# Turning the latents in 32x32 blocks on VectorE instead of on TensorE

## The reference, cut to what matters

```python
proj = jnp.einsum('bsd,dn->bsn', xn, w_in[l])
a_q, a_k, a_v, a_g, b_cq, b_ckv, b_kr, b_g = jnp.split(proj, _SPLITS, axis=-1)
...
c_q = rms_norm(b_cq, b_cq_norm[l])
c_kv = rms_norm(b_ckv, b_ckv_norm[l])
qb = jnp.einsum('bsr,rn->bsn', c_q, w_uq[l])
kvb = jnp.einsum('bsr,rn->bsn', c_kv, w_ukv[l])
...
h = h + jnp.einsum('bsm,md->bsd', y, w_out[l])
```

## Time and profile before

| | |
|---|---|
| median of 3 runs | 1583.99 us (1583.68 to 1584.9) |
| profiled execution | 1581.66 us, its span 1579.9 us |
| TensorE products | 1534.4 us busy, 97% of the span |
| TensorE weight loads | 889.6 us, 56% |
| VectorE | 1303.0 us, 82% |
| ScalarE | 1232.3 us, 78% |
| GpSimd | 586.0 us, 37% |
| mean granted clock of TensorE | 0.997 |

### The profile page before, as it was taken

One profiled execution on the slowest core, in us unless ns is written; L12 is line 12 of the kernel. 1 busy time (PEld: TensorE's weight loads), 2 busy tenths in 40 slices (PEclk: granted clock), 3 DMA queues, 4 the chain that ended last, 5 costly groups with the idle time before them and its releaser, 6 DMA issues.

```text
span 1579.9 us, 37686 instructions
## 1 busy us (share of the span) xinstructions
PE 1534.4 (97%) x13326; PEld 889.6 (56%) x13326; DVE 1303.0 (82%) x1947; ACT 1232.3 (78%) x1656; POOL 586.0 (37%) x506
## 2 busy tenths in 40 slices
PE   7999999999998999999999999999999999979999
PEld 3555555555553566566566556656655655644444
DVE  6886676776888988998898899899889889897764
ACT  8787667667657888888888888888888888877663
POOL 0100000000002665666666566666656656630000
PEclk9999999999999999999999999999999999999999
DMA  9344444453323543334323334323332422536663
GB/s 339 109 137 76 112 116 71 109 110 70 82 65 98 112 99 72 86 82 96 79 64 92 79 79 97 86 65 70 83 66 63 92 58 67 125 91 213 201 198 106
DMA packets 245540, 162.51 MB, mean 103 GB/s; under 512 B 65040, under 2 KB 226320, under 8 KB 245488
## 3 DMA queue, kind: packets, MB, share of 16 engines
q1 hardware_dynamic: 222128, 147.28, 37.2%
q10 hardware_dynamic: 22464, 13.63, 3.1%
q0 software_dynamic: 896, 0.93, 0.8%
HBM read 119.16 MB, written 40.93 MB: 101 GB/s over the span
## 4 chain that ended last, share of the span: by engine, by line
PE 56%; DVE 8%; issue 3%; ACT 0%; DVEq 0%; DMA 0%; POOLq 0%; SPq 0%
PE p_acc L2063 5%; PE p_st L2027 5%; PE p_st L2026 5%; PE p_acc L2067 4%; DVE hand_part L1864 4%; PE hand_mx L1994 4%; PE p_acc L2069 4%; PE p_acc L2068 3%; PE p_st L1507 3%; PE p_st L1508 3%; PE p_st L1510 3%; PE p_st L2029 3%; PE p_st L2030 3%; PE hand_mx L1996 3%; PE p_acc L2064 3%
## 5 line engine op out<-in xcount | busy, mean ns | idle before, releaser
L1776 POOL TENSOR_TENSOR p_pl<-p_p,p_ph 128x512 f16<-128x512 f32 x384 | 503.9, 1319 | 291.6 <-ACT p_ph L1815 232.3
L1864 DVE TENSOR_REDUCE hand_part<-hand_mx 128x2 f32<-128x1024 f32 x373 | 455.0, 1220 | 78.1 <-PE hand_mx L1994 60.0
L1806 ACT ACTIVATE p_p<-p_st 128x1024 f32<-128x1024 f32 x384 | 390.9, 1018 | 98.3 <-PE p_st L2034 50.2
L1194 PE MATMUL p_ring<-p_w_hi,p_xT 128*128 128x512 f16 (+3 forms) x1536 | 389.3, 339 | 7.5 <-DVE p_w_lo L902 5.0
L1815 ACT ACTIVATE p_ph<-p_p 128x1024 f16<-128x1024 f32 x336 | 355.2, 1057 | 18.4
L1892 DVE TENSOR_TENSOR p_pl<-p_p,p_ph 128x512 f16<-128x512 f32 x384 | 325.9, 849 | 5.4 <-ACT p_ph L1815 4.6
L1194 PE MATMUL p_ring<-p_w_lo,p_xT 128*128 128x512 f16 (+3 forms) x768 | 260.0, 339 | 0.0
L1194 PEld LDWEIGHTS p_ring<-p_w_hi,p_xT 128*128 128x128 f16 x1536 | 150.7, 98 | 127.1 <-DVE p_xT L860 5.6
L2063 PE MATMUL p_acc<-p_vas,p_ph 128*128 128x129 f16 x2048 | 207.9, 221 | 0.0
L2063 PEld LDWEIGHTS p_acc<-p_vas,p_ph 128*128 128x128 f16 x2048 | 180.6, 97 | 36.4 <-issue 14.1
L2064 PE MATMUL p_acc<-p_vas,p_pl 128*128 128x65 f16 x2048 | 201.1, 193 | 0.0
(11 more groups left out here) (196 smaller groups left out, 2364.8 us busy)
## 6 DMA issues: line engine op xcount, KB each, us to landing
p_vbs<-scratch_vb SPq DMA_DIRECT2D x16, 1028.0 KB, 6.3
p_xin<-in_x SPq DMA_DIRECT2D x16, 512.0 KB, 7.1
p_xcol<-in_x_cols SPq DMA_DIRECT2D x16, 512.0 KB, 6.7
scratch_g<-p_g SPq DMA_DIRECT2D x16, 512.0 KB, 3.4
p_kb<-scratch_kb SPq DMA_DIRECT2D x32, 256.0 KB, 5.4
p_vas<-in_x SPq DMA_DIRECT2D x16, 512.0 KB, 4.0
out<-p_ph SPq DMA_DIRECT2D x15, 512.0 KB, 2.8
out_gt<-scratch_g ACTq DMA_DIRECT2D x13, 512.0 KB, 3.4
```

The source lines that it names most:

```text
L1194: last = pe.matmul(ring_t[:, 0:w], a, b, start=(k == 0 and m == 0), stop=(k == len(steps) - 1 and m == len(terms) - 1))
L1776: pool.tensor_tensor(pl[:, s % NP, 1, :], p32[:, s % N32, QB:], ph[:, s % NP, 1, :], ALU.subtract).then_inc(s_lop, 1)
L1806: act.activation(p32[:, s % N32, :], st[:, s % 2, :, :].rearrange("p a b -> p (a b)"), ACT.Exp, scale=scale).then_inc(s_exp, 1)
L1864: dve.tensor_reduce(part[:, e // MPAIRS % 3, 2 * c:2 * c + 2], mx[:, :, :], AX, ALU.max).then_inc(s_red, 1)
```

## The change

The latents are scaled in float32 in place (`latent_scale`, ScalarE), turned in 32x32 blocks by VectorE into `turned_lat`, a part of the tile `T2` that the rotation uses at other times (`latent_turn`), split into halves from there (`latent_hi`, `latent_lo`), and put in their places by 16 copies of 32x320, eight on each engine (`latent_move`). TensorE's `turn_latents`, the two copies from PSUM and their semaphores go. In ScalarE's queue `latent_hi` now stands behind `z_hi` and `latent_move` where `latents_turned` stood. In VectorE's, `latent_turn` stands where `latent_lo` stood, and `latent_lo` behind `x_lo`. In tiles 14 and 15 all but the moves stand ahead of `rotate_heads`.

```diff
-        lat_hi = sb("lat_hi", [P, RQ + RKV], F16)
-        lat_lo = sb("lat_lo", [P, RQ + RKV], F16)
+        lat = sb("lat", [P, 2, RQ + RKV], F16)
...
+        turned_lat = T2[:, 0:RQ + RKV]
...
-        turned_hi = ps("turned_hi", [P, 8, P], F16)
-        turned_lo = ps("turned_lo", [P, 8, P], F16)
+        turned_hi = ps("turned_hi", [P, 2, P], F16)
+        turned_lo = ps("turned_lo", [P, 2, P], F16)
...
+        def latent_moves(quadrants):
+
+            halves = lat[:, :, :].rearrange("p s (k q t) -> p (s k) q t", k=5, q=4)
+            for g, d in moves(quadrants):
+                yield latT[32 * d:32 * d + 32, :, 32 * g:32 * g + 32], halves[32 * g:32 * g + 32, :, d, :]
...
         def _(act):
-            def latents_turned(t):
-
-                act.wait_ge(s_lph, t + 1)
-                act.activation(latT[:, 0:5, :], turned_hi[:, 0:5, :], ACT.Copy).then_inc(s_lth, 1)
+            def latent_move(t):
+
+                act.wait_ge(s_dlat, t * 3 + 3)
+                if not zero(t):
+                    act.wait_ge(s_proj, turn(t - 1, "ukv1") + 1)
+                for dst, src in latent_moves((2, 3)):
+                    last = act.activation(dst, src, ACT.Copy)
+                last.then_inc(s_lta, 1)
...
+            def latent_scale(t, h):
                 ls = lstat[:, h, :]
-                act.wait_ge(s_dlat, t * 2 + 1)
+                act.wait_ge(s_dlat, t * 3 + 1)
+                act.activation(cq32[:, h, :], cq32[:, h, :], ACT.Copy, scale=ls[:, 4:5])
+                act.activation(ckv32[:, h, 0:RKV], ckv32[:, h, 0:RKV], ACT.Copy, scale=ls[:, 5:6]).then_inc(s_lat, 1)
+
+            def latent_hi(t):
+
+                act.wait_ge(s_dlat, t * 3 + 2)
                 if not zero(t):
-                    act.wait_ge(s_lph, t)
-                act.activation(lat_hi[:, 0:RQ], cq32[:, h, :], ACT.Copy, scale=ls[:, 4:5])
-                act.activation(lat_hi[:, RQ:], ckv32[:, h, 0:RKV], ACT.Copy, scale=ls[:, 5:6]).then_inc(s_lat, 1)
+                    act.wait_ge(s_lta, t)
+                    act.wait_ge(s_ltd, t)
+                act.activation(lat[:, 0, :], turned_lat, ACT.Copy).then_inc(s_lat, 1)
...
                 latent_stat(t, h)
-                latent_hi(t, h)
+                latent_scale(t, h)
                 if not last:
                     z_hi(t - 1, 1 - h)
+                    latent_hi(t)
                     x_hi(t + 1, 1 - h)
                     aq_out(t, h)
                     akv_out(t, h)
-                    latents_turned(t)
+                    latent_move(t)
                     z_move(t - 1, 1 - h, i if h == 1 else i - 1)
                     gate(t, "ag")
                 elif h == 0:
+                    latent_hi(T14)
                     aq_out(T14, 0)
                     akv_out(T14, 0)
                     z_hi(T13, 1)
-                    latents_turned(T14)
+                    latent_move(T14)
                     z_move(T13, 1, PAIRS - 2, quadrants=(3,))
                     x_hi(T15, 1)
                     gate(T13, "bg")
                 else:
                     akv_out(T15, 1)
                     last_k_sq()
+                    latent_hi(T15)
                     aq_out(T15, 1)
                     last_k_dev()
                     k14_hi()
-                    latents_turned(T15)
+                    latent_move(T15)
                     z_hi(T14, 0)
                     last_k_hi()
...
         def _(dve):
-            def latents_turned(t):
-
-                dve.wait_ge(s_lpl, t + 1)
-                dve.tensor_copy(latT[:, 5:10, :], turned_lo[:, 0:5, :]).then_inc(s_ltl, 1)
+            def latent_move(t):
...
+                for dst, src in latent_moves((0, 1)):
+                    last = dve.tensor_copy(dst, src)
+                last.then_inc(s_ltd, 1)
...
+            def latent_turn(t, h):
+
+                dve.wait_ge(s_lat, t * 6 + 5)
+                dve.transpose(turned_lat[:, 0:RQ], cq32[:, h, :])
+                dve.transpose(turned_lat[:, RQ:], ckv32[:, h, 0:RKV]).then_inc(s_dlat, 1)
+
+            def latent_lo(t):
+
+                dve.wait_ge(s_lat, t * 6 + 6)
                 if not zero(t):
-                    dve.wait_ge(s_lpl, t)
...
+                    dve.wait_ge(s_lta, t)
+                dve.tensor_tensor(lat[:, 1, :], turned_lat, lat[:, 0, :], ALU.subtract).then_inc(s_dlat, 1)
...
                 x_scale(t + 1, 1 - h)
-                latent_lo(t, h)
+                latent_turn(t, h)
                 z_lo(t - 1, 1 - h)
                 x_lo(t + 1, 1 - h)
+                latent_lo(t)
...
-                latents_turned(t)
+                latent_move(t)
...
                 if h == 0:
+                    latent_turn(T14, 0)
                     x_scale(T15, 1)
-                    latent_lo(T14, 0)
+                    latent_lo(T14)
+                    dve.wait_ge(s_dlat, T14 * 3 + 3)
                     rotate_heads(T13, 1)
+                    latent_move(T14)
                     z_lo(T13, 1)
-                    latents_turned(T14)
...
                 else:
+                    latent_turn(T15, 1)
+                    latent_lo(T15)
+                    dve.wait_ge(s_dlat, T15 * 3 + 3)
                     rotate_heads(T14, 0)
-                    latent_lo(T15, 1)
+                    latent_move(T15)
                     last_k_sum()
                     k14_lo()
                     last_k_chain()
                     last_k_lo()
-                    latents_turned(T15)
...
         def _(pe):
-            def turn_latents(t):
...
             def up(t, new):
-                pe.wait_ge(s_lth, t + 1)
-                pe.wait_ge(s_ltl, t + 1)
+                pe.wait_ge(s_lta, t + 1)
+                pe.wait_ge(s_ltd, t + 1)
```

More of the change, by code:

```diff
@@ L722, in last_k_turned @@
                 act.wait_ge(s_kp, 1)
-                act.activation(zT[:, 4, :], turned_hi[:, 5:7, :].rearrange("p b t -> p (b t)"), ACT.Copy).then_inc(s_kta, 1)
+                act.activation(zT[:, 4, :], turned_hi[:, :, :].rearrange("p b t -> p (b t)"), ACT.Copy).then_inc(s_kta, 1)
             def v_hi(t):
@@ L757, in first_pair @@
                 split_hi(4, 0)
-                latent_hi(0, 0)
+                latent_scale(0, 0)
                 cq_out(1, 1)
                 split_hi(4, 1)
+                latent_hi(0)
                 ckv_out(1, 1)
                 latent_stat(1, 1)
-                split_all(5)
+                split_hi(5, 0)
+                latent_move(0)
+                split_hi(5, 1)
                 aq_out(0, 0)
-                latents_turned(0)
-                latent_hi(1, 1)
+                latent_scale(1, 1)
                 x_stat(2, 0)
@@ L770, in first_pair @@
                 split_hi(6, 0)
+                latent_hi(1)
                 up_out(0, 0)
@@ L878, in z_move @@
                 last.then_inc(s_ztd, 1)
-            def latents_turned(t):
-                dve.wait_ge(s_lpl, t + 1)
-                dve.tensor_copy(latT[:, 5:10, :], turned_lo[:, 0:5, :]).then_inc(s_ltl, 1)
+            def latent_move(t):
+                dve.wait_ge(s_dlat, t * 3 + 3)
+                if not zero(t):
+                    dve.wait_ge(s_proj, turn(t - 1, "ukv1") + 1)
+                for dst, src in latent_moves((0, 1)):
+                    last = dve.tensor_copy(dst, src)
+                last.then_inc(s_ltd, 1)
             def k14_lo():
@@ L910, in latent_rstd @@
                 ls = lstat[:, h, :]
-                dve.wait_ge(s_lat, t * 5 + 4)
+                dve.wait_ge(s_lat, t * 6 + 4)
                 dve.reciprocal(ls[:, 4:6], ls[:, 2:4]).then_inc(s_dlat, 1)
[L914 to L917, removed]
-                if not zero(t):
-                    dve.wait_ge(s_lpl, t)
[L920 to L923, removed]
+            def latent_turn(t, h):
[4 more added lines that the diff above has]
+                dve.wait_ge(s_lat, t * 6 + 6)
+                if not zero(t):
+                    dve.wait_ge(s_lta, t)
+                dve.tensor_tensor(lat[:, 1, :], turned_lat, lat[:, 0, :], ALU.subtract).then_inc(s_dlat, 1)
             def heads_sum(t):
@@ L1098, in first_pair @@
                 split_lo(4, 0)
-                latent_lo(0, 0)
+                latent_turn(0, 0)
                 split_lo(4, 1)
+                latent_lo(0)
                 latent_rstd(1, 1)
-                split_all(5)
-                latents_turned(0)
-                latent_lo(1, 1)
+                split_lo(5, 0)
+                latent_move(0)
+                split_lo(5, 1)
+                latent_turn(1, 1)
                 x_rstd(2, 0)
                 split_all(6)
+                latent_lo(1)
                 split_lo(7, 0)
@@ L1109, in first_pair @@
                 v_lo(0)
[L1110 removed]
+                latent_move(1)
                 split_lo(7, 1)
@@ L1210, in rstd_rows @@
                 pe.transpose(rsp[:, t, :], stat[:, t, 2:3].to_broadcast([P, P]), eye32[:, :]).then_inc(s_rsp, 1)
-            def turn_latents(t):
```

(24 more changed lines are left out.)

20 lines of the change are left out of this document (6 added, 14 removed).

## The result

| | before | after |
|---|---|---|
| median | 1583.85 us (1583.68 to 1584.9, 4 runs) | 1644.67 us (1641.66 to 1647.0, 4 runs) |
| profiled execution | 1581.66 us | 1647.0 us, its span 1645.2 us |
| mean granted clock of TensorE | 0.997 | 0.984 |

What follows compares the result with a forecast made beforehand. TensorE's queue was taken to bound the first phase. Waits of 49.5 us, with the 8.8 us win already in, and 14 us of clock make 63.5: 1581.7 becomes 1645.2, plus 2.3 for the median, 1647; range 1612 to 1666.

Steps and rivals of the forecast that it cites:

- Where TensorE would stand: Between ukv0 and ukv1, once a tile, TensorE waits 3.3 us for ScalarE's copy of ag.
- (b): Partly hidden: cheaper moves or turns make the ag copy late by only 0.8 us; 1604 to 1614, chance 0.10.
- (c): Faster: ScalarE's moves end before ag's copy is wanted, 8.8 us come off the regular tiles; about 1576, chance 0.05.
- (e): TensorE is relieved but nothing moves, the additions and the 8.8 us cancelling; 1584, chance 0.03.
- (d): Worse: VectorE's turns at their upper bound, dearer scaling, longer end stalls, clock low after each stall; about 1666, chance 0.08.
- The loop without the clock: Reciprocal, turn, moves, ag copy, ukv1, squares, head chain, reciprocal: closes in 31.8 us a tile with no slack.
- nine tiles at 2.8: Tiles 3 to 11 each cost 2.8 us more against 28.97 before, entered as +25.0.
- the 476.4 of tile 15: Time in us when the last key's low half, which TensorE waits for, is ready in tile 15; before, 469.0.
- the forecast's clock term: Low clock after stalls: 1.0 us for each of tiles 2 to 13, 2 us in tile 15; 14 us, bounds 0 and 22.
- the upper bound of 1.7: The most a stretch of 3.4 us at low clock behind a TensorE stall can cost, in us.
- rival (a): The clock holds: the same waits but no clock term of 14 us; 1633, chance 0.22.
- the sums of +4.0 and +5.3: Added us: +4.0 in tile 14, moves ahead of x_hi and a gate copy; +5.3 in tile 2, later latent moves.

Runs made afterwards that it cites:

- the second experiment: The changed kernel with all sixteen latent moves on VectorE and none on ScalarE; 1600.76 us, ratio 1.0093.
- the filling: The changed kernel with 42 unread products of 128 columns put into TensorE's stall between ukv0 and ukv1 in tiles 2 to 13; 1637.64 us, ratio 1.0327.
- the mixed kernel: Tiles 0 to 3, 14 and 15 as in the kernel before, tiles 4 to 13 in blocks with all sixteen moves on VectorE; 1578.49 us, ratio 0.9962.
- the reordered kernel before: The kernel before with ScalarE's four wide head moves put behind the roots of the heads in tiles 2 to 13; 1609.4 us, ratio 1.0158.

## Why the prediction was right, step by step

**Where TensorE would stand: right.** ukv1 waits for the gate copy 13 times, 35.6 us in all. The stall was put at 3.3 us and is 3.1. Half of the moves taken away gave back 1.9 us, all on VectorE the whole loss of the middle tiles; with that rivals (b), (c) and (e) fall, and with the durations below (d), which wanted the turns at their upper bound. The mechanism of (c), moves that end before the copy is wanted, is real once ScalarE has none of them: the second experiment's 28.41.

**The durations: right within 0.1 us.** Turns 0.57 and 0.41 us (put at 0.58 and 0.45), moves 3.81 and 1.96 (3.8 and 1.9), subtraction 0.82. The loop without the clock is 31.7 (31.8). The ten turns are worth 0.56 us a tile (0.55). Two slips of the sum are small: nine tiles at 2.8 are 25.2, not 25.0, and VectorE's own copy from PSUM, 0.49 us a tile before, also goes, which changes nothing while VectorE waits 8 us. How the 476.4 of tile 15 comes about is not written out.

**The places**, in the shift of the squares against before; the forecast's clock term of 1.0 a tile is added to its values (2 for the last):

| tiles | forecast | measured |
|---|---|---|
| 0 and 1 | 4.7 | 5.2 |
| 2 | 6.3 | 6.0 |
| 3 to 11 | 34.0 | 32.4 |
| 12 and 13 | 6.5 | 7.6 |
| 14 | 4.0 | 5.1 |
| 15 | 8.0 | 8.5 |
| all | 63.5 | 64.9 |

The rows here are one execution each, 1647.0 against 1581.66 us; the medians lie 60.8 us apart. That the forecast of the median (1647, measured 1644.67) is as close as that of the execution (1645.2, measured 1647.0) is in part luck: I added 2.3 us because the median lay above the profiled execution before, and after the change it lies 2.3 us below.

**The clock: the sum right, its shape wrong.** I took 1.0 us after every stall. In the middle tiles the trace has 1.5 us after every second one and nothing after the others, 0.8 in the mean; over tiles 3 to 13 that makes the 10.8 us that the filling gave back, where I had 11. The price lay near the upper bound of 1.7, and half of the stalls paid it. That the two made up for each other is luck. So rival (a), a clock that holds, was half true, and falls as a whole: the filling experiment took 8.6 us away.

The step behind it was wrong as well. I compared the lengths of stalls: 3.3 us was nearest to the 3.29 that had been followed by a fall, and 2.34 stood for none. The length does not decide. These rows of the windows view are, in this order, the stretches right behind five stalls: of 2.34 us in tile 15, in the kernel before and in the mixed kernel; of 3.84 us in tile 14, in the changed kernel and with the stall of the middle tiles filled; of 3.58 us in tile 7 of the reordered kernel before.

```profile
464.90:468.30 3.40, 3.38 (x20) 1.73 (x21) 2.56 (x13) 2.44 (x5) 0.00 (x0) 1.00 0.00 1
460.50:463.90 3.40, 3.37 (x12) 1.57 (x13) 2.56 (x13) 2.44 (x5) 0.00 (x0) 0.50 0.05 16
499.34:502.70 3.36, 2.61 (x15) 1.39 (x15) 0.38 (x1) 3.30 (x7) 0.00 (x0) 1.00 0.00 0
486.90:490.30 3.40, 3.40 (x12) 1.67 (x13) 0.43 (x1) 3.34 (x7) 0.00 (x0) 0.54 0.00 0
260.30:263.70 3.40, 3.34 (x17) 1.68 (x18) 0.16 (x1) 3.26 (x10) 0.00 (x0) 1.00 0.33 130
```

The same stall of the same length is followed by the full clock in one kernel and by half of it in another. The Trainium skill, "TensorE: Matmul & The Clock Gate", section on the HAM clock gate, says that the monitor runs freely and does not start anew when a kernel does. That would fit stalls of one length with two outcomes, but no run here varied the moment of a stall and nothing else, so why it is exactly each second tile stays open.

**Tile 15: right in size and in kind.** TensorE's timeline of after, last tile:

```profile
532.32 0.37 PE L1251 MATMUL p_turned_hi<-hand_ident,p_junk 128*128 128x128 f16 x2 [8.52 <-ACT p_junk L730]
532.56 0.39 PE L1255 MATMUL p_turned_lo<-hand_ident,p_junk 128*128 128x128 f16 x2
532.75 0.53 PE L1228 MATMUL p_ring<-p_uq_hi,p_latT 128*128 128x384 f16 x1
...
556.00 0.38 PE L1228 MATMUL p_ring<-p_w_hi,p_xT 128*128 128x512 f16 x1
```

About 9 us of idle time were forecast and 8.52 came; the products of 384 columns behind it start 0.32 us apart, where 0.16 is the rate at the full clock. They do so until 538.2, so the low clock cost some 2.7 us here, where I had taken 2; the waits alone are then 5.8, for a forecast of 6.0. ScalarE shows who is late:

```profile
495.48 3.81 ACT L632 ACTIVATE p_latT<-p_lat 32x320 f16<-32x320 f16 x8
...
501.24 1.06 ACT L596 ACTIVATE p_xT<-p_xcol 128x1024 f16<-128x1024 f32 x1
...
526.16 0.29 ACT L722 ACTIVATE p_rstat<-p_rstat,p_eps 128x2 f32<-128x2 f32 x1 [6.91 <-DVE p_rstat L1075]
...
526.68 3.81 ACT L632 ACTIVATE p_latT<-p_lat 32x320 f16<-32x320 f16 x8
```

The roots of the last key (526.16) wait 6.91 us for VectorE, which first turns, splits, rotates and moves. In tile 14 the moves (495.48) stand ahead of x_hi (501.24). What I had not written down is a stall in that tile ahead of uq, 3.84 us for ScalarE's latent moves, and one of 4.44 us in tile 2: in the middle tiles the moves end just in time, at the ends they don't. Its cost was inside the sums of +4.0 and +5.3, but reached through the gate copy and x_hi.

**The turn on TensorE or on VectorE.** The Trainium skill, "VectorE: DVE Perf Modes", Rules for kernel authors, prefers TensorE for a whole turn if the result may go to PSUM. The change as made bears it out, though not by the duration that its table lists: 0.56 us a tile for ten turns is a seventh of what that would give. What costs is the copies that put VectorE's blocks in their places. In the middle tiles, where VectorE has time for all sixteen of them, turning in blocks was the faster way (28.41 against 28.97 us).

## What to carry to other kernels

Before work goes from a full engine to one with free time, look up what stands behind it in the new queue: ScalarE had 9.5 us free in a tile, but between reading akv and reading ag it had 0.8 to spare, and 3.8 us went there. Price removed instructions by the distance between the starts of their neighbours, not by their own bars (ten turns: 0.55 us, not 2.2), and look at the first and last rounds of a loop by themselves: with all moves on VectorE the middle gained 6 us and the ends lost 24. The length of a stall alone does not tell whether the clock falls behind it: price it by both bounds. When work is moved to a free place, ask also who stores its result, and when the next writer of that tile needs it back.

## What the runs showed of the hardware

- Two stalls of 3.08 and 3.11 us, with TensorE busy ahead of both, were followed once by the full clock and once by 3.4 us at 0.52, at a price of 1.5 us. The stalls of 2.5 us in tiles 12 and 13 were each followed by a fall, a stall of 2.34 us in one kernel of two, while one of 3.84 and one of 3.58 us were followed by none, so the length alone does not decide. Stalls of 1.2 to 1.3 us, and the 0.75 to 0.9 us that the filling leaves, never were in tiles 3 to 11.
- Ten transposes of 128x128 in float16 in a full queue of TensorE take 0.55 us of it, 0.056 each, though each row shows 0.22.
- A copy of 32x320 in float16 from one quadrant to another takes 466 ns on ScalarE and 232 on VectorE, and eight in a row take 3.81 us on the one and 1.96 on the other.
- VectorE turns 32x32 blocks of float32 in 0.57 us for 384 columns and 0.40 us for 256 (means of 16); with the 1.65 us for 1408 I estimate some 1.05 ns a column and a fixed part of 0.13 to 0.17 us.
